# Hybrid attention encoder layer: the input projection, apart from the near values, computed from feature pairs as seven block products

## The chip, the core and the metric

The kernel runs on one core of one Trainium2 chip. Its engines are TensorE (PE, matrix products; its weight loads are listed as PEld), VectorE (DVE), ScalarE (ACT), GpSimd (POOL) and SyncE (SP), which here only starts transfers. Each engine works through its own list of instructions in order, and a wait on a semaphore holds up everything behind it on that engine. The metric is the device time of one execution in microseconds.

## The reference

One encoder layer on x of 2048 tokens by 1024 features, float32. What the change touches is the first part:

```python
h = rmsnorm(x, g_norm_mix[l])
proj = h @ w_in[l]                       # 2048x1024 by 1024x2304
qa, ka, va, qb, kb, vb = jnp.split(proj, split_at, axis=-1)
...
qb = partial_rope(qb.reshape(b, s, SWA_HEADS, HEAD_DIM), pos)   # first 16 of 64 dims
kb = partial_rope(kb.reshape(b, s, SWA_KV_HEADS, HEAD_DIM), pos)
oa = neighbourhood_attention(qa, ka, va, na_rpb[l])   # 8 heads, 2-D windows
ob = windowed_gqa_sink(qb, kb, vb, swa_sink[l])       # 8 query heads, 2 key heads
...
x = x + o @ w_out[l]
x = x + (silu(h @ w_gate[l]) * (h @ w_up[l])) @ w_down[l]
```

qa, ka and va ("near") are 512 features each, qb ("window" queries) is 512, kb and vb are 128 each.

## The kernel before

Every large product is made from float32 operands split into a high part (rounded to the fast float32 format of PE, by ACT) and a low part (the rest, by DVE), and three matmuls replace one: high by high, high by low, low by high. All matmuls of the projection have 128 rows of output and 512 columns, or 256.

The work goes in stages: projection, attention (8 rounds of two heads), output projection with the norm after it ("mix"), and the feed-forward part. Order on each engine is written out by hand; no scheduler moves anything. The projection (`project_phase`, L60) has three stages of its own.

**Near values, token by token.** For each of 16 tiles of 128 tokens, ACT sums the squares (L375), DVE makes the norm's factor and the normed tile (L455 to L462), PE turns it with eight 128x128 transposes (L541), ACT and DVE split the turned tile into `hT` (L370, L450), and PE makes 24 matmuls against the 512 value columns (`token_step`, L573 to L575). ACT copies the result (L412), SP and POOL store it. PE's list is: product of tile t, transposes of tile t + 2, product of tile t + 1.

**Near queries and keys, feature-major.** 32 steps j of 24 matmuls each (L600 to L602): 128 features by 512 tokens. ACT and DVE split each result (L430, L515, L517), SP stores both parts to `qk_scratch` (L299). `w_out` is scaled and split on the side, one of eight pieces every second step.

**Window keys and values, then window queries, token by token.** 16 steps of 16 matmuls and 16 steps of 24 matmuls. The rotation is done with tokens on the partitions, on 16 of each head's 64 columns (`rope`, L470 to L484: four short DVE instructions a tile), and PE turns the result back (`turn_tok`, L551: one or four 128x128 transposes a tile). In the same stage SP loads what attention needs first: the queries, keys and values of heads 0 and 1, between the steps (`load_ahead`, L258).

The feed-forward part (`feed_phase`, L1484) already computes its products as seven block products of sums instead of eight (`product`, L2058). It alternates between two weight matrices, so that consecutive products on PE belong to different chains.

## Time and profile before

| | us |
|---|---|
| median of 3 runs | 2220.44 (2219.46 to 2220.89) |
| profiled execution, first to last instruction | 2218.6 |
| PE busy in it | 2185.7 (99%) |
| DVE busy | 1427.1 (64%) |
| ACT busy | 929.7 (42%) |
| POOL busy | 233.5 (11%) |

The profiled execution has no time of its own beside its span; the span is 1.8 us under the median of the runs, which is what lies around it (before the first and after the last instruction). Times of a stage are read as us from the span's start. A matmul's duration (389 ns) is longer than the distance between two starts, since matmuls overlap in the array; the distance is what counts on PE. The same holds for back-to-back work of DVE and ACT to a lesser degree.

### The profile page before, as it was taken

Reading aid. Unit: us, or ns where it says so; the run is one execution under the profiler, and the core shown is the slowest. Engines: PE = TensorE matmul, PEld = TensorE weight load, DVE = VectorE, ACT = ScalarE, POOL = GpSimd, SP = SyncE. Lnnn points to the kernel's source line nnn. Section 1 sums busy time; section 2 is a strip of 40 time slices with the busy share of each in tenths; the row PEclk is TensorE's granted clock in tenths of the full one; section 3 lists DMA queues with packets and bytes.
Section 4 is the critical chain, followed back from the end, with each engine's and each line's share of the span. In section 5 each row is a group of like instructions: output and inputs, shape, how many; then the busy total and the mean of one; then the engine's idle time right before and its main releaser. Section 6 shows DMA issues by size and latency. Waiting matters only on the chain.

```text
span 2218.6 us, 33179 instructions
## 1 busy us (share of the span) xinstructions
PE 2185.7 (99%) x11464; PEld 1813.6 (82%) x11464; DVE 1427.1 (64%) x2767; ACT 929.7 (42%) x1834; POOL 233.5 (11%) x263
## 2 busy tenths in 40 slices
PE   8999999999999999999999999999999999999998
PEld 6888888788888888888888888888888887888887
DVE  4423142499888778776656568765656578575676
ACT  4423121388889643353333335333333334131343
POOL 2370001145100000011121111100000000000000
PEclk9999999999999999999999999999999999999999
DMA  7488425789974376665454558432232286353544
GB/s 229 143 241 276 148 87 155 201 221 250 222 207 142 110 229 218 232 210 194 151 196 165 196 174 302 149 118 96 92 122 81 102 321 223 114 180 103 193 147 154
DMA packets 278149, 393.46 MB, mean 177 GB/s; under 512 B 15530, under 2 KB 182578, under 8 KB 271616
## 3 DMA queue, kind: packets, MB, share of 16 engines
q1 hardware_dynamic: 269040, 366.73, 51.7%
q0 software_dynamic: 6528, 16.07, 2.4%
q10 hardware_dynamic: 2448, 8.91, 1.5%
q8 instruction: 81, 1.33, 0.2%
q14 instruction: 52, 0.43, 0.1%
HBM read 246.16 MB, written 148.70 MB: 178 GB/s over the span
## 4 chain that ended last, share of the span: by engine, by line
PE 92%; DVE 4%; issue 1%; DMA 1%; ACT 1%; DVEq 0%; ACTq 0%
PE late_psum L2089 12%; PE late_psum L2090 12%; PE late_psum L2091 12%; PE late_psum L2115 6%; PE late_psum L2117 6%; PE late_psum L2116 6%; PE late_psum L1051 4%; PE late_psum L1028 4%; PE late_psum L1433 3%; PE late_psum L573 3%; PE late_psum L575 3%; PE late_psum L574 3%; PE late_psum L1435 3%; PE late_psum L1434 3%; PE late_psum L601 3%; PE late_psum L600 3%
## 5 line engine op out<-in xcount | busy, mean ns | idle before, releaser
L2089 PE MATMUL late_psum<-ff_h,ff_ring 128*128 128x512 f32 x1232 | 479.6, 389 | 1.3 <-DVE ff_acts L1950 1.3
L2090 PE MATMUL late_psum<-ff_h,ff_ring 128*128 128x512 f32 x1232 | 479.3, 389 | 0.0
L2091 PE MATMUL late_psum<-ff_h,ff_ring 128*128 128x512 f32 x1232 | 479.3, 389 | 0.0
L2089 PEld LDWEIGHTS late_psum<-ff_h,ff_ring 128*128 128x128 f32 x1232 | 231.3, 188 | 50.1 <-DVE ff_acts L1950 2.2
L2090 PEld LDWEIGHTS late_psum<-ff_h,ff_ring 128*128 128x128 f32 x1232 | 231.3, 188 | 48.0
L2091 PEld LDWEIGHTS late_psum<-ff_h,ff_ring 128*128 128x128 f32 x1232 | 231.3, 188 | 47.8
L2115 PE MATMUL late_psum<-ff_d,ff_a 128*128 128x512 f32 x616 | 240.0, 390 | 2.1 <-DVE ff_x L2008 1.4
L2117 PE MATMUL late_psum<-ff_d,ff_a 128*128 128x512 f32 x616 | 239.7, 389 | 0.0
L2116 PE MATMUL late_psum<-ff_d,ff_a 128*128 128x512 f32 x616 | 239.7, 389 | 0.0
L2008 DVE TENSOR_TENSOR ff_x<-late_psum,ff_x 128x512 f32<-128x512 f32 x224 | 153.3, 690 | 117.1 <-PE late_psum L2117 116.5
L1908 DVE TENSOR_TENSOR ff_ring<-ff_raw,ff_ring 128x512 fp32r<-128x512 f32 x176 | 130.7, 744 | 103.2 <-ACT ff_ring L1785 103.0
L914 ACT ACTIVATE att_probs<-att_neg_scores,att_negmax 128x385 f32<-128x385 f32 (+4 forms) x256 | 161.1, 629 | 22.8 <-DVE att_negmax L962 21.9
L1800 ACT CAST ff_a<-ff_a 128x768 fp32r<-128x768 f32 (+2 forms) x96 | 81.5, 878 | 206.3 <-DMA ff_a<-acts_scratch 206.1
L1908 DVE TENSOR_TENSOR ff_ring<-ff_sums,ff_ring 128x512 fp32r<-128x512 f32 x132 | 94.5, 717 | 112.4 <-ACT ff_ring L1785 112.1
L1785 ACT CAST ff_ring<-ff_raw 128x512 fp32r<-128x512 f32 x176 | 109.3, 623 | 137.1 <-PE late_psum L2091 135.9
L1028 PE MATMUL late_psum<-ident,att_probs 128*128 128x128 f32 (+1 forms) x816 | 133.8, 277 | 10.9 <-ACT att_probs_turned L936 4.9
L2115 PEld LDWEIGHTS late_psum<-ff_d,ff_a 128*128 128x128 f32 x616 | 115.6, 188 | 27.5 <-issue 2.1
L2117 PEld LDWEIGHTS late_psum<-ff_d,ff_a 128*128 128x128 f32 x616 | 115.6, 188 | 24.1
L2116 PEld LDWEIGHTS late_psum<-ff_d,ff_a 128*128 128x128 f32 x616 | 115.6, 188 | 24.0
L936 ACT COPY att_probs_turned<-late_psum 128x384 f32<-128x384 f32 (+2 forms) x256 | 124.4, 487 | 19.1 <-PE late_psum L1028 19.0
L1028 PEld LDWEIGHTS late_psum<-ident,att_probs 128*128 128x128 f32 (+1 forms) x816 | 98.5, 140 | 39.8 <-issue 16.3
L975 DVE TENSOR_SCALAR att_probs<-att_probs,att_rtotal 128x384 f32<-128x384 f32 (+3 forms) x256 | 129.9, 508 | 0.1
(151 smaller groups left out, 3934.1 us busy)
## 6 DMA issues: line engine op xcount, KB each, us to landing
acts_scratch<-ff_acts SPq DMA_DIRECT2D x22, 1792.0 KB, 8.2
ff_a<-acts_scratch SPq DMA_DIRECT2D x24, 960.0 KB, 5.2
ff_raw<-in_w_gate SPq DMA_DIRECT2D x44, 512.0 KB, 3.8
ff_raw<-in_w_up SPq DMA_DIRECT2D x44, 512.0 KB, 4.0
ff_d<-down_scratch SPq DMA_DIRECT2D x21, 768.0 KB, 6.5
att_q_stack<-qk_scratch SPq DMA_DIRECT2D x56, 256.0 KB, 6.1
ffn_in_scratch<-mix_h_stage SPq DMA_DIRECT2D x8, 1792.0 KB, 6.2
ff_h<-ffn_in_scratch SPq DMA_DIRECT2D x14, 1024.0 KB, 8.4
```

Source lines behind the costliest of these rows:

```text
L914: nc.scalar.activation(pr[:, i, lo:hi], sn[:, i, lo:hi], ACT.Exp, bias=negmax[:, i:i + 1], scale=-1.0, accum_out=total[:, i:i + 1]).then_i ...
L936: nc.scalar.copy(turned_buffer(u)[:, 0:n], tp[:, u % 2, 0:n]).then_inc(pt_copied, 1)
L975: nc.vector.tensor_scalar(pr[:, i, c0:c0 + n], pr[:, i, c0:c0 + n], rtotal[:, i:i + 1], None, ALU.mult).then_inc(probs_done, 1)
L1028: last = pe.transpose(tp[0:rows, u % 2, j * P:(j + 1) * P], pr[:, i, c0 + j * P:c0 + j * P + rows], ident[:])
L1908: nc.vector.tensor_tensor(ff.ring[m % TURNS][:, 1], weight_of(m), ff.ring[m % TURNS][:, 0], ALU.subtract) \
L2008: nc.vector.tensor_tensor(to, down_bank(e, j), to, ALU.add).then_inc(added, 1)
L2089: pe.matmul(out_bank, whi[:, k], hhi[:, :, k], start=(k == 0 and not onto), stop=False, skip_group_check=onto)
L2090: pe.matmul(out_bank, whi[:, k], hlo[:, :, k], start=False, stop=False, skip_group_check=onto)
L2091: last = pe.matmul(out_bank, wlo[:, k], hhi[:, :, k], start=False, stop=(k == 3), skip_group_check=onto)
L2115: pe.matmul(bank, hi, dhi, start=(i == 0 and not onto), stop=False, skip_group_check=onto)
L2116: pe.matmul(bank, hi, dlo, start=False, stop=False, skip_group_check=onto)
L2117: last = pe.matmul(bank, lo, dhi, start=False, stop=(i == n - 1), skip_group_check=onto)
```

## The change

The 1792 feature columns of w_in that are not near values are reordered on the host side of the launch into seven pairs of 128 + 128 (`pair_columns`), and the input projection for them becomes a 2x2 block product: contraction halves by feature halves by token halves. Such a block product is made with seven products of sums and differences (Strassen-Winograd) instead of eight. There are 14 groups g (7 pairs for the first half of the tokens, the same 7 for the second), each with seven products j of 12 matmuls of 128x512: 98 products n = 7g + j. Pair 0 and part of pairs 1 and 2 are window queries; pair 1 also has the window keys, pair 2 the window values, pairs 3 to 6 are near queries with near keys.

- The near-value stage stays, tile by tile, in another order of tiles, but it now also makes the sums of the turned input: ACT copies parts of the turned tile (`turn_copy`), and after every second tile DVE makes four sums (`turn_sums`). For the second half of the tokens the seven operands (1792 KB for each pair of tiles) go to DRAM and come back for group 7. The seven operands of a half are split into high and low in pieces of 128x2048 (`split_hi`, `split_lo`), seven of these for the second half.
- The sums of weights are made by DVE (`weight_sums`, `last_weight_sum`: four of 128x512 a group). POOL's queue loads the weights, 1 MB a group. `pair_hi` and `pair_lo` split the weights of one product, six products ahead.
- Results are put together from partial sums: ACT copies three of them out of PSUM (`evacuate`), DVE adds to them (`join`), then ACT and DVE split the four results of a group (`result_hi`, `result_lo`).
- The rotation is done with features on the partitions: window queries are grouped so that one 128-row result holds 16 dimensions of all eight heads, and DVE makes a shuffle of partitions, two products with tables and a sum, all of 128x512 (`rope`, four times in groups 1 and 8). SP loads the tables, two of four parts at a time. The 80 transposes of rotated tiles go; 16 transposes of window values come (`turn_values`).
- `w_out` is scaled from product 59 on, one piece every four products.
- The first loads of attention move behind product 91 and later ones (`first_loads`), in smaller pieces; the last projection tile is no longer finished inside attention's first steps, and the identity matrix is no longer loaded again.

Where three places of the lists stood before, and stand now. First, DVE at the end of the near-value stage: `hT` and `x_turned` are the turned and split tile, `x_normed` the normed tile, `proj_h_stage` the sums of the turned input. Before:

```order
L450 TENSOR_TENSOR hT<-late_psum,hT 128x1024
L455 TENSOR_SCALAR msq<-ssq 128x1
L458 RECIPROCAL inv<-msq 128x1
L462 SCALAR_TENSOR_TENSOR x_normed<-x_tile,rstd,g_mix_rows 128x1024
L450 TENSOR_TENSOR hT<-late_psum,hT 128x1024
L467 TENSOR_TENSOR w_lo<-w_raw,w_hi 128x1024 x4
```

After, for an odd tile:

```order
L632 TENSOR_TENSOR x_turned<-late_psum,x_turned 128x512 x2
L641 TENSOR_TENSOR proj_h_stage<-late_psum,proj_h_stage 128x512
L642 TENSOR_TENSOR proj_h_stage<-proj_h_stage,late_psum 128x512
L644 TENSOR_TENSOR proj_h_stage<-proj_h_stage 128x512
L646 TENSOR_TENSOR proj_h_stage<-proj_h_stage 128x512
L650 TENSOR_SCALAR msq<-ssq 128x1
L653 RECIPROCAL inv<-msq 128x1
L657 SCALAR_TENSOR_TENSOR x_normed<-x_tile,rstd,g_mix_rows 128x1024
```

The four sums now stand between the low part of one tile and the norm of the next.

Second, the rotation. SP before, at the window keys and values: `v_window_scratch` is the store of values, `stage` holds the split results.

```order
L299 DMA qk_scratch<-stage_hi 128x512
L299 DMA qk_scratch<-stage_lo 128x512
L322 DMA v_window_scratch<-x_tile 128x128
L333 DMA qk_scratch<-stage_hi 128x128
L333 DMA qk_scratch<-stage_lo 128x128
L255 DMA w_raw<-in_w_in 128x2x512
```

SP after, in group 1: stage 2 holds the second result of the group (the window keys), stage 0 the third.

```order
L331 DMA qk_scratch<-stage_hi1 8x16x512
L331 DMA qk_scratch<-stage_lo1 8x16x512
L331 DMA qk_scratch<-stage_hi2 128x512
L331 DMA qk_scratch<-stage_lo2 128x512
L294 DMA rope_rows0<-in_rope 128x2x512 x2
L331 DMA qk_scratch<-stage_hi0 8x16x512
L331 DMA qk_scratch<-stage_lo0 8x16x512
```

And DVE there (c1 is the third result, c3 the second):

```order
L697 TENSOR_TENSOR proj_c1<-late_psum,proj_c1 128x512
L671 TENSOR_TENSOR proj_ring0<-proj_raw0,proj_ring0 128x512
L727 TENSOR_TENSOR stage_lo2<-proj_c3,stage_hi2 128x512
L711 STREAM_SHUFFLE rope_swapped0<-proj_c1 128x512
L713 TENSOR_TENSOR rope_swapped0<-rope_swapped0,rope_rows0 128x512
L714 TENSOR_TENSOR proj_c1<-proj_c1,rope_rows0 128x512
L716 TENSOR_TENSOR proj_c1<-proj_c1,rope_swapped0 128x512
```

The tables, loaded by POOL's queue before, are now between two stores on SP, and the third rotation stands right behind the low part of the second result.

Third, DVE where the second half of the tokens is prepared. Before, in the near keys (L517 is a result's low part, L467 a weight split, L247 a piece of `w_out`):

```order
L515 TENSOR_TENSOR stage_lo<-late_psum,stage_hi 128x8x4x16
L467 TENSOR_TENSOR w_lo<-w_raw,w_hi 128x8x128
L517 SCALAR_TENSOR_TENSOR stage_lo<-late_psum,stage_hi 128x512
L247 SCALAR_TENSOR_TENSOR w_out_parts<-w_out_raw,g_out,w_out_parts 128x1024
L517 SCALAR_TENSOR_TENSOR stage_lo<-late_psum,stage_hi 128x512 x4
```

After, in products 45 to 47 (`proj_h_second` is an operand of the second half, `ring` the split weights, c3 and c1 results):

```order
L667 TENSOR_TENSOR proj_h_second<-proj_h_second 128x2048
L697 TENSOR_TENSOR proj_c3<-late_psum,proj_c3 128x512
L671 TENSOR_TENSOR proj_ring4<-proj_w_sums,proj_ring4 128x512
L667 TENSOR_TENSOR proj_h_second<-proj_h_second 128x2048
L729 SCALAR_TENSOR_TENSOR stage_lo1<-proj_c3,stage_hi1 128x512
L689 TENSOR_TENSOR proj_w_sums<-proj_raw0,proj_w_sums 128x512
L697 TENSOR_TENSOR proj_c1<-late_psum,proj_c1 128x512
L671 TENSOR_TENSOR proj_ring5<-proj_raw1,proj_ring5 128x512
L667 TENSOR_TENSOR proj_h_second<-proj_h_second 128x2048
L727 TENSOR_TENSOR stage_lo2<-proj_c1,stage_hi2 128x8x4x16
```

Three of the long splits stand in three consecutive products, among the joins that PE waits for.

The diff, cut to its core:

```diff
+    OP_LOADS = {8: 1, 23: 0}
+    OP_LOADS.update({PER_G * HALF_GROUPS - PER_G + o - 1: o for o in range(2, SEVEN)})
+    SPLIT_AT_TILE = {13: (0, 2), 14: (0, 3), 15: (0, 4)}
+    SPLIT_AT = {0: (0, 6), 24: (1, 1), 31: (1, 0), 45: (1, 2), 46: (1, 3), 47: (1, 4), 49: (1, 5), 51: (1, 6)}
...
+    HI_AT = {ROPED: (2, 5, 6, 8), VALUES: (1, 6, 5, 9)}
+    ROPE_AT = (1, 4, 5, 7)
+    SIDES = ((0, 0), (1, 1), (0, 1), (1, 0))
+    order = sorted(((PER_G * g + HI_AT.get(kind_of(g), (1, 4, 5, 6))[i], g, i) for g in range(G) for i in range(4)))
...
+    def store_sums(u):
+        sp.wait_ge(h_summed, 4 * (u + 1))
+        sp.dma_start(sums_dram[:, :, u - 4].rearrange("o p c -> p o c"), hs[:]).then_inc(h_stored, 16)
+    def load_rope(b, turn):
+        for side, half in enumerate((0, 1) if turn == 0 else (1, 0)):
+            if turn == 0 and b == 0:
+                sp.wait_ge(v_done, NT)
+            elif turn == 0:
+                sp.wait_ge(prod_done, PER_G * HALF_GROUPS)
+            else:
+                sp.wait_ge(roped, 4 * b + side + 1)
+            cols = slice((2 * b + half) * BANK, (2 * b + half + 1) * BANK)
+            sp.dma_start(mem.p_rope[b][:, side], rope_in_dram[side].rearrange("c p s -> p c s")[:, :, cols]) \
+                .then_inc(rope_in[side], 16)
...
+    def load_op(o):
+        if o == 1:
+            sp.wait_ge(h_stored, 64)
...
+        else:
+            sp.wait_ge(prod_done, HOME_FREED[o])
+        sp.dma_start(hc[:, o, 1].bitcast(F32), sums_dram[o].rearrange("p q c -> p (q c)")).then_inc(h_in[o], 16)
...
+    def first_loads(att):
+        sp.wait_ge(prod_done, PRODUCTS - 6)
+        for slot in range(STAGES):
+            sp.wait_ge(stored[slot], max(v for r, v in stored_by.items() if r % STAGES == slot and order[r][1] < G - 2))
+        att.load_q(att.near, 0, 0)
+        sp.wait_ge(prod_done, PRODUCTS - 4)
+        att.load_k(att.near, 0, 0)
+        att.load_k(att.near, 0, 1)
+        sp.wait_ge(prod_done, PRODUCTS - 3)
+        for half in range(2):
+            sp.wait_ge(v_stored[half], 32 * NT)
+            sp.wait_ge(v_stored_by_pool[half], 32 * NT)
+        att.load_v(att.near, 0, 0)
+        att.load_v(att.near, 0, 1)
+        att.load_k(att.near, 0, 2)
+        att.load_q(att.near, 0, 1)
...
+        load_rope(0, 0)
+        for n in range(LAST_STEP + 1):
+            if n == 7 * ROPED + 6:
+                load_rope(0, 1)
+            if n == PER_G * HALF_GROUPS:
+                load_rope(1, 0)
...
+            for r, g, i in results_at(n):
+                store_result(r, g, i)
+            if n == 95:
+                first_loads(att)
...
-    def turn_hi(t):
-        act.wait_ge(turned, t + 1)
-        nc.scalar.copy(hT[:, t, 0], tp[:, t % 2, :].rearrange("p (k s) -> p k s", k=KT)).then_inc(h_hi_done, 1)
+    def turn_hi(t):
+        act.wait_ge(turned, t + 1)
+        if t >= 8 or t in (5, 7):
+            act.wait_ge(v_done, slot_before(t) + 1)
+        for half in range(2):
+            last = nc.scalar.copy(raw_part(t, half, 0), tp[:, t % 2, half * BANK:(half + 1) * BANK])
+        last.then_inc(h_hi_done, 1)
...
+    def turn_copy(t):
+        u = t // 2
+        if t < 2:
+            act.wait_ge(h_lo_done, t + 1)
+        if t == 0:
+            act.wait_ge(v_lo_done, 4)
+        elif t % 2 == 0:
+            act.wait_ge(h_summed, 4 * u)
+            if u > 4:
+                act.wait_ge(h_stored, 16 * (u - 4))
+        if t % 2 == 0:
+            nc.scalar.copy(hs[:, 0:2], tp[:, 0].rearrange("p (o c) -> p o c", o=2)).then_inc(h_copied, 1)
+        else:
+            nc.scalar.copy(hs[:, 5], tp[:, 1, BANK:2 * BANK]).then_inc(h_copied, 1)
...
+    def pair_hi(n):
+        g, j = place(n)
+            act.wait_ge(sums_made, 4 * g + {2: 2, 3: 1, 4: 3, 5: 4}[j])
+        if RING // 2 <= n < RING:
+            act.wait_ge(v_done, NT)
+        if n >= RING:
+            act.wait_ge(prod_done, n - RING + 1)
+        nc.scalar.copy(ring[n % RING][:, 0], weight_of(n)).then_inc(w_hi_done, 1)
+    def evacuate(n):
+        g, j = place(n)
+        if j == 3 and g >= 1:
+            if kind_of(g - 1) == VALUES:
+                act.wait_ge(v_turned, 2 * (g // HALF_GROUPS) + 1)
+            else:
+                all_low(act, g - 1, 1)
+        act.wait_ge(prod_done, n + 1)
+        if j in (0, 2, 3):
+            nc.scalar.copy({0: c0, 2: c1, 3: c3}[j][:], bank_of(g, j)).then_inc(copied, 1)
...
-    def turn_lo(t):
-        dve.wait_ge(h_hi_done, t + 1)
-        nc.vector.tensor_tensor(hT[:, t, 1], tp[:, t % 2, :].rearrange("p (k s) -> p k s", k=KT), hT[:, t, 0],
-                                ALU.subtract).then_inc(h_lo_done, 1)
+    def turn_sums(u):
+        t = 2 * u + 1
+        s3, s4, s2, s6 = (sum_of(t, o) for o in (3, 4, 2, 6))
+        dve.wait_ge(h_copied, t + 1)
+        nc.vector.tensor_tensor(s3, tp[:, 1, 0:BANK], hs[:, 0], ALU.subtract).then_inc(h_summed, 1)
+        nc.vector.tensor_tensor(s4, hs[:, 5], tp[:, 1, 0:BANK], ALU.subtract).then_inc(h_summed, 1)
+        dve.wait_ge(h_summed, 4 * u + 1)
+        nc.vector.tensor_tensor(s2, hs[:, 5], s3, ALU.subtract).then_inc(h_summed, 1)
+        dve.wait_ge(h_summed, 4 * u + 3)
+        nc.vector.tensor_tensor(s6, hs[:, 1], s2, ALU.subtract).then_inc(h_summed, 1)
...
+    def split_lo(b, o):
+        nc.vector.tensor_tensor(op_of(b, o)[:, 1], op_sums(b, o), op_of(b, o)[:, 0], ALU.subtract).then_inc(op_lo_done, 1)
...
+    def weight_sums(g):
+        nc.vector.tensor_tensor(sums[:, 0], a21, a22, ALU.add).then_inc(sums_made, 1)
+        dve.wait_ge(sums_made, 4 * g + 1)
+        nc.vector.tensor_tensor(sums[:, 1], sums[:, 0], a11, ALU.subtract).then_inc(sums_made, 1)
+        nc.vector.tensor_tensor(a21, a11, a21, ALU.subtract).then_inc(sums_made, 1)
...
+    def join(n):
+        g, j = place(n)
+        first, to = {1: (1, c0), 4: (3, c3), 5: (2, c1)}[j]
+        dve.wait_ge(copied, 3 * g + first)
+        dve.wait_ge(prod_done, n + 1)
+        nc.vector.tensor_tensor(to[:], bank_of(g, j), to[:], ALU.add).then_inc(summed, 1)
...
-        nc.vector.tensor_tensor(rope_c[:, 0:heads, :], v[:, :, 0:ROPE], cos, ALU.mult).then_inc(rope_step, 1)
-        nc.vector.tensor_tensor(rope_s[:, 0:heads, 0:HALF], v[:, :, HALF:ROPE], sin[:, :, 0:HALF],
...
-        nc.vector.tensor_tensor(v[:, :, 0:ROPE], rope_c[:, 0:heads, :], rope_s[:, 0:heads, :],
...
+    def rope(g, i):
+        dve.wait_ge(rope_in[side], 16 * (2 * b + (1 if i < 2 else 2)))
+        nc.vector.stream_shuffle(swapped[:], v[:], [lane ^ 8 for lane in range(32)]).then_inc(rope_step, 1)
+        dve.wait_ge(rope_step, 3 * nth + 1)
+        nc.vector.tensor_tensor(swapped[:], swapped[:], table[:, side, 1], ALU.mult).then_inc(rope_step, 1)
+        nc.vector.tensor_tensor(v[:], v[:], table[:, side, 0], ALU.mult).then_inc(rope_step, 1)
+        dve.wait_ge(rope_step, 3 * nth + 3)
+        nc.vector.tensor_tensor(v[:], v[:], swapped[:], ALU.add).then_inc(roped, 1)
...
+        for n in range(LAST_STEP + 1):
+            g, j = place(n)
+            if n < PRODUCTS and j in (1, 4, 5):
+                join(n)
+            if n + RING < PRODUCTS:
+                pair_lo(n + RING)
+            if n in SPLIT_AT:
+                split_lo(*SPLIT_AT[n])
+            for r, gg, i in results_at(n):
+                result_lo(r, gg, i)
+            for gg, i in ropes_at(n):
+                rope(gg, i)
+            if j == 2 and g + 1 < G:
+                weight_sums(g + 1)
+            if j == 4 and g + 1 < G:
+                last_weight_sum(g + 1)
+            if n - 2 in OUT_AT:
+                out_weights_lo(OUT_AT[n - 2])
...
-            for k in range(KT):
-                if j == 0:
-                    wait_low(pe, 4 + k // 2)
-                pe.matmul(mm[:, j % 4, :], w_hi[:, k, cols], hT[:, tiles, 0, k, :], start=(k == 0), stop=False)
-                pe.matmul(mm[:, j % 4, :], w_hi[:, k, cols], hT[:, tiles, 1, k, :], start=False, stop=False)
-                last = pe.matmul(mm[:, j % 4, :], w_lo[:, k, cols], hT[:, tiles, 0, k, :], start=False,
+    def product(n):
+        g, j = place(n)
...
+        if g >= 2 and j in (1, 3):
+            pe.wait_ge(summed, 3 * (g - 2) + {1: 1, 3: 3}[j])
+        if j in (2, 4, 5):
+            pe.wait_ge(copied, 3 * g + {2: 1, 4: 2, 5: 3}[j])
+        if j == 6:
+            pe.wait_ge(summed, 3 * g + 2)
+        pe.wait_ge(w_lo_done, n + 1)
...
+        for k in range(4):
+            pe.matmul(out, whi[:, k], hhi[:, :, k], start=(k == 0 and not onto), stop=False, skip_group_check=onto)
+            pe.matmul(out, whi[:, k], hlo[:, :, k], start=False, stop=False, skip_group_check=onto)
+            last = pe.matmul(out, wlo[:, k], hhi[:, :, k], start=False, stop=(k == 3), skip_group_check=onto)
```

## Rows read from the trace of the kernel before

**Rows 1.** The page: span, and engines of the chain of work that ended last.

```profile
span 2218.6 us, 33179 instructions
...
PE 92%; DVE 4%; issue 1%; DMA 1%; ACT 1%; DVEq 0%; ACTq 0%
```

**Rows 2.** Busy time by stage: span, PE, PEld, DVE, ACT, POOL, PEclk, DMA, GB/s.

```profile
291.00:435.00 144.00, 143.30 (x731) 120.44 (x729) 51.85 (x186) 32.07 (x73) 8.23 (x8) 1.00 0.58 156
435.00:447.00 12.00, 9.20 (x54) 7.17 (x55) 10.99 (x37) 8.64 (x26) 5.42 (x5) 0.72 0.34 88
```

**Rows 3.** Timeline of PE: start, duration, instruction; transposes, then first product of the queries.

```profile
66.63 1.03 PE L541 MATMUL late_psum<-ident,x_normed 128*128 128x128 f32 x8
...
72.96 1.04 PE L541 MATMUL late_psum<-ident,x_normed 128*128 128x128 f32 x8
...
116.49 0.39 PE L600 MATMUL late_psum<-hT,w_hi 128*128 128x512 f32 x1
```

**Rows 4.** Timeline of PE where attention begins.

```profile
430.84 0.60 PE L551 MATMUL late_psum<-ident,x_tile 128*128 128x128 f32 x4
431.19 0.41 PE L1015 MATMUL late_psum<-att_k_stack,att_q_stack 128*128 128x352 f32 x1
...
437.08 0.55 PE L1028 MATMUL late_psum<-ident,att_probs 128*128 128x128 f32 x3 [2.27 <-DMA ident<-in_ident]
```

**Rows 5.** Timeline of PE in the feed-forward products.

```profile
1002.06 0.39 PE L2089 MATMUL late_psum<-ff_h,ff_ring 128*128 128x512 f32 x1
...
1002.74 0.39 PE L2089 MATMUL late_psum<-ff_h,ff_ring 128*128 128x512 f32 x1
```

**Rows 6.** Timeline of ACT, one tile of the near values.

```profile
66.82 0.59 ACT L412 COPY stage_hi<-late_psum 128x512 f32<-128x512 f32 x1 [2.72 <-PE late_psum L575]
67.70 1.02 ACT L370 CAST hT<-late_psum 128x1024 fp32r<-128x1024 f32 x1 [0.29 <-PE late_psum L541]
...
68.61 1.06 ACT L375 ACTIVATE x_normed<-x_tile 128x1024 f32<-128x1024 f32 x1
```

**Rows 7.** Timeline of DVE, the same tile.

```profile
68.75 1.23 DVE L450 TENSOR_TENSOR hT<-late_psum,hT 128x1024 fp32r<-128x1024 f32 x1 [3.33 <-ACT hT L370]
...
70.07 0.17 DVE L458 RECIPROCAL inv<-msq 128x1 f32<-128x1 f32 x1
70.50 1.29 DVE L462 SCALAR_TENSOR_TENSOR x_normed<-x_tile,rstd,g_mix_rows 128x1024 f32<-128x1024 f32 x1 [0.27 <-ACT rstd L377]
```

**Rows 8.** Timeline of DVE, back-to-back work of 128x512 in the feed-forward products.

```profile
1019.79 0.68 DVE L1935 TENSOR_TENSOR ff_gate<-late_psum,ff_gate 128x512 f32<-128x512 f32 x1
1020.39 0.68 DVE L1908 TENSOR_TENSOR ff_ring<-ff_raw,ff_ring 128x512 fp32r<-128x512 f32 x1
```

**Rows 9.** Groups of instructions on DVE, 860 to 1400 us: the split of 128x2048.

```profile
L1913 DVE TENSOR_TENSOR ff_h<-ff_h 128x2048 fp32r<-128x2048 f32 x14 | 33.1, 2364 | 7.8 <-ACT ff_h L1789 7.8
```

**Rows 10.** Timeline of ACT in the feed-forward products.

```profile
1008.43 0.59 ACT L1811 COPY ff_gate<-late_psum 128x512 f32<-128x512 f32 x1 [1.61 <-PE late_psum L2091]
1008.92 0.62 ACT L1785 CAST ff_ring<-ff_raw 128x512 fp32r<-128x512 f32 x1
```

**Rows 11.** DMA issues up to 440 us: count, KB each, median us to landing.

```profile
w_raw<-in_w_in SPq DMA_DIRECT2D x18, 512.0 KB, 6.9
x_tile<-in_x ACTq DMA_DIRECT2D x16, 512.0 KB, 4.3
```

**Rows 12.** DMA issues of the whole page.

```profile
ffn_in_scratch<-mix_h_stage SPq DMA_DIRECT2D x8, 1792.0 KB, 6.2
```

**Rows 13.** Timeline of SP: the issue of one load of keys.

```profile
404.65 0.60 SPq L840 DMA_DIRECT2D att_k_stack<-qk_scratch  x1
```

**Rows 14.** Timeline of DVE in attention's first steps.

```profile
433.19 0.52 DVE L962 CUSTOM_DVE_ANT_0 att_neg_scores<-late_psum,bias 128x352 f32<-128x352 f32 x1
...
435.12 1.51 DVE L975 TENSOR_SCALAR att_probs<-att_probs,att_rtotal 128x352 f32<-128x352 f32 x1
...
441.64 0.40 DVE L975 TENSOR_SCALAR att_probs<-att_probs,att_rtotal 128x352 f32<-128x352 f32 x1
```

938 lines of the change are left out of this document (510 added, 428 removed).

## The prediction

> **What bounds the kernel now.** Read the page's head and chain first: PE is on 92% of the chain that ended last [rows 1], so a change pays only if it takes time out of PE's list, and costs whatever it makes PE wait. Then the busy time by stage: from 291 to 435 us, the stage of the rotated features, PE is busy 143.3 of 144.0 us, DVE 51.9 and ACT 32.1 [rows 2]. There PE never waits; the others have two thirds of the time free. Then the timelines, for what one instruction costs back to back. Two starts of the same line of a product are 0.68 us apart, which is three matmuls of 512 columns [rows 5]: 0.227 us each, so a product of 12 takes 2.72 us and one of 24 takes 5.44. DVE's instructions of 128x512 start 0.60 us apart and end 0.68 after their start [rows 8]; ACT's start 0.49 apart and last 0.6 [rows 10]; DVE's split of 128x2048 takes 2.36 [rows 9]. ACT's of that size is not shown; its 1024 columns take 1.02 [rows 6], so 2.05. I add 0.04 for a handover between engines: ACT's result is read by DVE 0.03 after its end [rows 6, 7].
>
> **What goes from PE's list.** The first product of the queries starts at 116.49, attention's first score at 431.19 [rows 3, 4]: 314.7 us. In its place stand 98 products of 2.72 us, 266.6, and 16 transposes; four of these take 0.35 us before the next row [rows 4], 1.5 in all. Saved, if PE never waits: 46.6 us. Everything else is what PE waits for.
>
> **The near-value stage.** A tile takes PE 6.33 us [rows 3]: eight transposes, 0.87, and 5.44. Let the value product of an odd tile t end at 0. PE turns tile t + 2, whose rows are there at 0.91 (ACT starts on them 0.88 after the start of its copy of the values, [rows 6]). ACT: two halves until 1.9, its copy of 512 until 2.4, the squares of tile t + 3 (0.96 and a read of the sum) until 3.5. DVE: two low halves from 2.45 until 3.7; four sums, two of which wait for the one before, until 6.2; then the norm: mean and inverse 0.35, ACT's root, and the 1.29 of the last step, which starts 0.43 after the inverse did [rows 7]: 8.1. PE wants to turn tile t + 3 at 6.33: it waits 1.8 us. In an even tile the sums are missing and the copy is twice as long: 6.0, in time. Odd tiles with a tile left to norm: t = 1, 3 to 11, six: 10.8 us. For the second half of the tokens the staged sums are also stored, 1792 KB, and ACT's next copy of an even tile waits for it. A store of this size lands 6.2 us after its issue [rows 12]; issued at 6.3, it is down at 12.5, where ACT wants to go on at 10.0 (the delay above included): 2.4 us more, for three tiles, 7.2. **18.0 us** together. Lower end 8 (the sums slip into gaps, only the stores wait), upper end 28 (each wait and landing half as long again).
>
> **Into the products.** DVE comes out of the tiles with three splits of 2.36, three weight sums and six weight splits. Counted from the end of tile 13, the last weight split that ACT must make before it copies the result of product 0 out waits for a sum DVE finishes at 18.2; the copy ends at 19.4, product 2 was due at 17.3; product 4 waits 1.8 more behind ACT. **3.9 us** (0 to 8).
>
> **A plain group.** Seven products are 19.0 us. DVE has seven weight splits, three joins, four sums, four low parts: 18 x 0.60 = 10.8; ACT 14 x 0.50 = 7. Followed through their lists step by step, with each one's waits for the other, both keep up; the join behind product 4 ends 0.7 after it, product 6 wants it at 2.7. Nothing, and `w_out`'s pieces (1.3 us on DVE each fourth product) fit as well.
>
> **The two rotation groups.** Counted from the end of product 8. The third rotation stands on DVE right behind the low part of the second result, which ends at 15.6. Its table is asked for by SP only after SP has stored that low part: issue at 16.5, and 512 KB land 4.3 us (tiles of x) to 6.9 us (weights) later [rows 11]; I take 5.5. So DVE starts it at 22, and is through at 24.8. (A rotation is a shuffle and three instructions with two handovers; no row shows a shuffle. It is bounded by 0.17, a one-column instruction, and 2.36, the one of 2048 [rows 7, 9]; I take the 0.68 of its own size, 2.8 for a rotation.) ACT stands behind it: high part of the third result 25.4, one weight split, and only then the copy of product 14's result, 26.4. Product 16, which adds onto that bank, was due at 19.1: PE waits 7.3 us, and 0.9 more before product 18. Twice, with two pieces of `w_out` in the second one that cost 1.0 before the transposes of values: **17.4 us** (5, if the tables are down in time and only DVE's load counts, to 24).
>
> **Splits of the second half's operands.** Products 24 and 31 each get one split of 2.36 on DVE ahead of a join: 0.7 us each. Products 45, 46, 47, 49 and 51 get five. Counted from the end of product 43, DVE is through with step 45 at 11.0, with step 46 at 18.5, with step 47 at 25.4, and ACT, which waits for each join, copies product 49's result out only at 24.1; product 51 was due at 19.9. Waits of 0.7, 4.3, 2.3, 0.4 and 2.2 at products 48, 51, 53, 54 and 55. With the first two: **11.3 us** (3 to 18).
>
> **Into attention.** Before, queries and keys lay ready, and DVE took the first score 2.0 us after PE's first [rows 4, 14]. Now SP comes to these loads after the store of the result of product 95, 1.4 us before the last product ends, and each issue takes 0.60 [rows 13]. Ten stand up to the last key the first score needs: the last is issued 4.6 us after the last product, and lands some 4.8 later (between 4.3 and 6.9, [rows 11]): 9.4, which is 7.4 later than before. Given back: the bias sums of POOL, under which DVE's scaling took 1.51 us for 0.40 [rows 14], are nearly over by then, about 3 us, and the last tile's low part 0.6. **+3.8 us** (0 to 8).
>
> **The sum.** 46.6 saved; 18.0 + 3.9 + 17.4 + 11.3 + 3.8 = 54.4 lost: 7.8 us slower. Against the profiled span of 2218.6 that is 2226.4; the runs' median lies 1.8 above the span: 2228.2. The terms' ends give 16 to 86 us lost, which all together is unlikely.
>
> **Rivals.** *The queues take it up* (faster). Handovers are shorter and the tables land before DVE wants them: then the rotation groups cost 5 and the splits, spread by PE's own lag, 4: 12.4 + 7.3 less, about 12 us faster, 2208. For it: DVE is idle two thirds of that stage now [rows 2], and its total load in the products, some 70%, leaves room. Against: PE's tolerance is one product, 2.7 us, since all seven belong to one chain, and the order of SP's list fixes the late table. *Half of it*: one of these two goes away but not the other, 2216 to 2225, taken as 2220. *The clock falls* (slower still). After PE's idle 2.27 us before 437.08 [rows 4] the stretch to 447 has a granted clock of 0.72 [rows 2], that is 0.56 of it, 6.7 us, at 1.2 GHz and the rest at 2.4. The change makes six waits of 2.3 us and more inside PE-bound work (three stores, two tables, one at product 51). If each is followed by 6.7 us at half clock, each costs up to 3.4 more, less where DVE is what is late: some 15 us, 2243. Against: the waits of the near-value stage stand between long products, and the wait before 437 is a single case. The Trainium skill ("TensorE: Matmul & The Clock Gate", section "HAM oscillation — how this bites in real kernels") says that waits between bursts of matmuls put the array back to half clock each time; by that rule this rival would be the forecast. The trace agrees for the wait before 437. That the change would not do what it says has no place here: the products are counted in the list.
>
> **Chances.** Forecast (2222 to 2236) 0.40; the clock falls 0.17; half of it 0.20; the queues take it up 0.23. A difference under 0.2% (4.4 us) is no change here. The forecast is slower but for 0.02 at its lower end, and the clock's case wholly; the last is faster; "half of it" is 0.18 no change and 0.01 to either side: faster 0.24, same 0.20, slower 0.56. The forecast's own range is 2222 to 2236; to hold eight in ten the range reaches to the rivals on both sides: 2207 to 2243.
>
> **What would show it.** Right: about 266.6 us of product time in 98 products at 0.227 a matmul; PE waits of about 1.8 us before the transposes of every second tile, larger from tile 10 on; DVE idle for about 6 us on a transfer of `rope_rows` before the third shuffle of each rotation group; a wait of 4 us before product 51; PE idle for about 9 us before the first score, waiting for `att_k_stack`. Wrong: no wait on `rope_rows` (SP reaches the load earlier than I count, or it lands faster), or near-value tiles that stay at 6.33; either alone takes the time towards no change, both make it faster. Granted clock under 1.00 between 20 and 420 us would speak for the fourth case.

## The result, and the profile after

The changed kernel takes 2267.22 us (median of 4 runs, 2266.05 to 2269.49) against 2220.32 for the kernel before in the same comparison (2219.46 to 2220.89): ratio 1.0214, 95% interval 1.0200 to 1.0229. The forecast was 2228 with 2207 to 2243 as its range, so the sign was right, and the size was short by 39 us. The profiled span is 2266.0 us, 47.4 more than before. The page's chain answers to [rows 1]:

```profile
PE 80%; DVE 7%; DMA 5%; issue 3%; ACT 3%; SPq 1%; DVEq 0%; ACTq 0%
```

PE had 92% of that chain; 12 points of it now belong to others. Busy time by stage answers to [rows 2] (span, PE, PEld, DVE, ACT, POOL, PEclk, DMA share, GB/s); the stretches are most of the near values, the two halves of the products, the gap before attention, and its start:

```profile
23.00:141.00 118.00, 101.09 (x444) 81.38 (x443) 58.20 (x100) 50.66 (x96) 29.77 (x59) 0.90 0.56 169
147.00:300.00 153.00, 140.83 (x606) 114.67 (x605) 101.74 (x149) 66.63 (x107) 44.86 (x76) 0.97 0.71 218
300.00:460.00 160.00, 139.13 (x579) 112.12 (x578) 103.26 (x151) 66.86 (x107) 5.47 (x7) 0.94 0.72 238
462.00:474.00 12.00, 0.21 (x1) 0.00 (x0) 1.15 (x2) 1.88 (x2) 12.00 (x11) 0.64 0.98 209
474.00:520.00 46.00, 36.84 (x298) 30.89 (x299) 31.84 (x114) 30.49 (x81) 15.63 (x15) 0.87 1.09 254
```

PE, which before had no idle time in the products, now stands still for 12.2 and 20.9 us of their two halves, and the granted clock is under 1.00 in every stretch. Three marks divide the 47.4. The first product starts at 146.72, where 116.49 stood [rows 3]: 30.2 later. The first score comes at 474.17, against 431.19 [rows 4]: 43.0. By the 40th score 48.2 us are lost, and from there to the end it stays between 47.7 and 48.2. So the near-value stage costs 30.2, the products nearly nothing net (+0.8 up to the start of their last row), and the start of attention 12.0 and then 5 more.

PE's rows with their waits, in the near-value stage, in the products and in attention:

```profile
85.53 1.12 PE L792 MATMUL late_psum<-ident,x_normed 128*128 128x128 f32 x8 [1.92 <-DVE x_normed L657]
95.94 1.29 PE L792 MATMUL late_psum<-ident,x_normed 128*128 128x128 f32 x8 [2.22 <-DVE x_normed L657]
...
202.32 0.80 PE L853 MATMUL late_psum<-proj_h_first,proj_ring 128*128 128x512 f32 x1 [8.09 <-ACT proj_c L540]
307.36 0.47 PE L853 MATMUL late_psum<-proj_h_second,proj_ring 128*128 128x512 f32 x1 [3.87 <-issue]
358.31 0.79 PE L853 MATMUL late_psum<-proj_h_second,proj_ring 128*128 128x512 f32 x1 [7.73 <-ACT proj_c L540]
372.51 0.50 PE L853 MATMUL late_psum<-proj_h_second,proj_ring 128*128 128x512 f32 x1 [3.60 <-ACT proj_c L540]
427.14 0.50 PE L853 MATMUL late_psum<-proj_h_second,proj_ring 128*128 128x512 f32 x1 [2.83 <-ACT proj_c L540]
474.17 0.63 PE L1243 MATMUL late_psum<-att_k_stack,att_q_stack 128*128 128x352 f32 x1 [11.96 <-issue]
...
499.07 0.76 PE L1243 MATMUL late_psum<-att_k_stack,att_q_stack 128*128 128x480 f32 x1 [5.18 <-DMA att_q_stack<-qk_scratch]
```

These are the waits the prediction named, nearly all at its places: about 1.9 before every second tile (4, 6, 8 and 10), larger ones from the stores on (tiles 11, 13 and 15), 8 before products 16 and 65 (counted from 0), 3.9 before product 51. All waits of about 0.4 us and more in the near-value stage add up to 17.3 (18.0 forecast, with a wait on ACT of 0.4), those in the products to 32.8 (32.6 forecast). And still 27 us more are gone: 12.9 in the near-value stage (30.2 less 17.3), for which a granted clock of 0.90 over 123.7 us has 12.4, and 14.2 in the products, whose 315.1 us are 268.1 of work at 0.227 us a matmul, 32.8 of waits and this rest, at a clock of 0.94 to 0.97.

Tile by tile it shows: behind the wait before tile 4 the clock falls, behind that before tile 6 it does not. The same work takes 7.98 us in the first and 6.42 in the second (one line for each, same columns):

```profile
37.83:45.81 7.98, 7.98 (x32) 6.59 (x33) 2.80 (x5) 3.24 (x6) 2.29 (x4) 0.79 0.82 259
54.24:60.66 6.42, 6.42 (x33) 5.30 (x33) 2.80 (x5) 3.24 (x6) 1.35 (x3) 1.00 0.58 161
```

That is where one is tempted to stop: the rival "the clock falls" seems to be the whole answer. The experiments say that it is a part, and a smaller one than 27 us.

### The profile page after: what moved, and what is told of

Its sections match the earlier page's. It is cut to its first block, busy times and chain, and to the rows that moved or that the text cites. A ratio compares the mean times of both kernels' runs of the same rounds, so it can differ in the third digit from the quotient of the medians.

```text
span 2266.0 us, 33068 instructions
## 1 busy us (share of the span) xinstructions
PE 2166.6 (96%) x11168; PEld 1787.7 (79%) x11168; DVE 1565.9 (69%) x2892; ACT 1012.7 (45%) x1967; POOL 243.7 (11%) x275
## 4 chain that ended last, share of the span: by engine, by line
PE 80%; DVE 7%; DMA 5%; issue 3%; ACT 3%; SPq 1%; DVEq 0%; ACTq 0%
PE late_psum L2334 11%; PE late_psum L2336 11%; PE late_psum L2335 11%; PE late_psum L2360 6%; PE late_psum L2361 6%; PE late_psum L2362 6%; PE late_psum L1278 4%; PE late_psum L1255 3%; PE late_psum L1676 3%; PE late_psum L1678 3%; PE late_psum L1677 3%; PE late_psum L853 2%; PE late_psum L855 2%; PE late_psum L854 2%; PE late_psum L1243 2%
## 5 line engine op out<-in xcount | busy, mean ns | idle before, releaser
L2030 ACT CAST ff_ring<-ff_sums 128x512 fp32r<-128x512 f32 x132 | 81.5, 619 | 113.6 <-PE late_psum L2336 108.2
L1243 PE MATMUL late_psum<-att_k_stack,att_q_stack 128*128 128x384 f32 (+3 forms) x256 | 112.5, 439 | 19.4 <-issue 12.0
```

What stands on the lines that cost most here:

```text
L1243: pe.matmul(out, q, kind.keys(k_st[:, e, 0, :], t), start=True, stop=False)
L2030: nc.scalar.copy(ff.ring[m % TURNS][:, 0], weight_of(m)).then_inc(w_hi_done, 1)
```

## Experiments

**Two repairs that each take away one thing.** Theory: VectorE's order costs the 1.9 us, the clock behind them the rest. In the first run the norm goes ahead of the sums:

```
             turn_lo(t + 2)
-            if t % 2:
-                turn_sums((t + 2) // 2)
         if t + AHEAD < NT:
             normed_tile(t + AHEAD)
+        if t + 2 < NT and t % 2:
+            turn_sums((t + 2) // 2)
```

> The changed kernel, with VectorE's order in the near-value stage turned round: the norm of tile t+3 ahead of the four sums of the pair (t+1, t+2). Theory A (waits and clock): the four waits of 1.9 us before the transposes of tiles 4, 6, 8 and 10 go (7.7 us), and with them most of what the clock lost in that stage (the first product is 30.2 us later than before, 17.3 of it waits and 12.4 half clock): 2251 (2247 to 2257), first product at about 131. Theory B (waits alone, the granted clock of that stage has another cause): 2259 (2257 to 2261) and a mean granted clock there that stays at 0.90. Theory C (the sums now make the copies and the 1792 KB stores later, and the three waits at tiles 11, 13 and 15 grow by as much): 2267.

Measured: 2266.56 us (ratio to before 1.0211, 1.0194 to 1.0228): no change. Theory C. Up to 80 us the stage has no wait over 0.5 us and a granted clock of 1.00, but then PE stands 8.4, 8.3 and 6.6 us, and the first product comes at 147.45. ACT's copies of an even tile and SP's stores of that kernel:

```profile
84.64 1.01 ACT L489 COPY proj_h_stage<-late_psum 128x1024 f32<-128x1024 f32 x1 [8.47 <-DMA proj_in_scratch<-proj_h_stage]
107.84 1.01 ACT L489 COPY proj_h_stage<-late_psum 128x1024 f32<-128x1024 f32 x1 [8.40 <-DMA proj_in_scratch<-proj_h_stage]
```
```profile
76.07 0.39 SPq L282 DMA_DIRECT2D proj_in_scratch<-proj_h_stage  x1
98.24 0.38 SPq L282 DMA_DIRECT2D proj_in_scratch<-proj_h_stage  x1
```

Copy, sums, store, copy again is a ring through one buffer. Here it turns in 23.2 us (84.64 to 107.84), where PE wants a pair of tiles in 12.7 (twice the 6.33 of [rows 3]). The same two rows in the changed kernel:

```profile
91.66 1.02 ACT L489 COPY proj_h_stage<-late_psum 128x1024 f32<-128x1024 f32 x1 [3.90 <-DMA proj_in_scratch<-proj_h_stage]
110.35 1.01 ACT L489 COPY proj_h_stage<-late_psum 128x1024 f32<-128x1024 f32 x1 [3.53 <-DMA proj_in_scratch<-proj_h_stage]
```
```profile
102.77 0.38 SPq L282 DMA_DIRECT2D proj_in_scratch<-proj_h_stage  x1
```

18.7 us for a turn: 11.1 from the copy to the store's issue, 7.6 from there to the next copy. (The turn ahead of it takes 19.9, from a copy at 71.81, the one behind it 18.6, to a copy at 128.99.)

With the norm first the same two parts are 13.6 and 9.6 us. The first is longer for theory C's reason, the sums that come later, and for another that it did not name: behind a wait of 8.4 us PE's product runs at half clock (tile 11 takes 8.4 us for 6.4), and the sums wait for the turned tile behind it. Why the stores also took 2 us longer was not tested.

The second run leaves all waits and fills them:

```
             value_step(t)
+            if t + 2 in FILL:
+                if t + 1 >= 4:
+                    pe.wait_ge(tok_done, t - 2)
+                for _ in range(FILL[t + 2]):
+                    pe.matmul(mm[:, (t + 1) % 4, :], raw_part(t, 0, 0)[:, 0:P], w_hi[:, 0], start=True, stop=True)
```

> The changed kernel with nothing moved: only that TensorE, where it waited for x_normed in the near-value stage, does useless products of 128x512 instead (8 each before tiles 4, 6, 8 and 10, 10 before 11, 2 before 12, 15 before 13, 12 before 15; 71 in all, 16.1 us at 0.227 each; their sums are overwritten). Clock theory: the same length of work in the place of the waits, but TensorE isn't idle, so the granted clock of the stage goes back from 0.90 to 1.00 and some 12 us come back: 2255 (2252 to 2260). Waits theory (what isn't a wait is contention or slower work elsewhere, and the clock in the records is no cause): no change, 2267 (2265 to 2270).

Measured: 2267.79 us (1.0216, 1.0199 to 1.0233): no change. The stretches that answer to the first three of the windows above:

```profile
23.00:141.00 118.00, 111.12 (x533) 90.05 (x532) 61.24 (x103) 52.92 (x99) 31.03 (x62) 1.00 0.60 181
147.00:300.00 153.00, 139.66 (x596) 113.64 (x596) 101.70 (x151) 65.82 (x106) 41.98 (x71) 0.96 0.70 219
300.00:460.00 160.00, 140.96 (x572) 114.03 (x572) 101.52 (x147) 64.63 (x106) 8.15 (x9) 0.91 0.71 234
```

In the near-value stage the clock is back at its full level, and ACT's copies still come 19.3 us apart (87.57, 106.91). The first product is at 141.11, 3.5 to 5.6 us earlier than in three kernels whose near-value stage is the same without the fill (144.57, 145.34, 146.72). Against the changed kernel's 146.72, 1.0 of the 5.6 us stands before tile 4 already. 3.1 are won from tile 4 to tile 10, nearly all in tiles 4 and 8, which ran behind a fallen clock (7.98 and 8.01 us, now 6.42 and 6.41). From tile 10 on, where the ring turns, only 1.5 are won, though the granted clock of the changed kernel's last 61.2 us (0.86) has some 8.6 us there. So the clock costs its full price where nothing but PE is late, and in the ring it is mostly hidden.

At the end nothing is left of the 5.6 us, and that is not the near-value stage's doing. The products, which the edit does not touch, have the same waits (32.5 us) but a lower granted clock than in the changed kernel (0.96 and 0.91 for 0.97 and 0.94), and take 318.4 us in place of 315.1. Why the clock fell oftener there is open. So no change at the end does not say that the clock has no price.

**The store in two.** What the ring needs free for the next copy is 512 KB of the 1792:

```
+    def store_copies(u):
+        sp.wait_ge(h_copied, 2 * u + 1)
+        sp.dma_start(sums_dram[0:2, :, u - 4].rearrange("o p c -> p o c"), hs[:, 0:2]).then_inc(copies_stored, 16)
...
             if u > 4:
-                act.wait_ge(h_stored, 16 * (u - 4))
+                act.wait_ge(copies_stored, 16 * (u - 4))
+        elif u > 4:
+            act.wait_ge(h_stored, 16 * (u - 4))
```

> The norm ahead of the four sums on VectorE, and the 1792 KB store of a pair's sums in two: the two copied operands (512 KB) as soon as the first copy of the pair stands, the five others after the sums. The first copy of the next pair then waits only for the small store. Theory A (two limits, each of which hid the other: VectorE's order costs 1.9 us at every second tile, the store costs the pair's cycle its length): both waits go, a tile takes 6.4 us again, the first product is at 119 (117 to 122) instead of 146.7, and all but a few us of it reach the end: 2242 (2236 to 2250). Theory B (what is won there is waited for again in the products or at the start of the attention, as with the filled waits, where 5.6 us at the first product were 2.3 at the 400th score): 2256 to 2262.

> The store in two as in the run above, but VectorE's order left as it was. Theory A (two limits): the three long waits at tiles 11, 13 and 15 (8.4 us) go and two more of 1.9 us show at tiles 12 and 14, so the stage is 5 us shorter and its granted clock stays near 0.90: 2262 (2259 to 2265). Theory B (the store alone is the limit, and the order of VectorE only hides in it): as the run above.

Measured, both edits: 2241.97 us (1.0101, 1.0085 to 1.0118). Store in two alone: 2258.90 (1.0169, 1.0152 to 1.0186), first product at 136.43. With norm first alone at 2266.56, that is 25 us for both, 8 and 0 for each: two limits, of which each hides the other. In the kernel with the store in two alone no ring is in the way, and all six waits of the prediction stand there, 1.9 each, before tiles 4, 6, 8, 10, 12 and 14. Behind four of them the clock falls and the tile takes 8.0 us, behind tiles 8 and 14 it does not and takes 6.4. Tiles 12 and 14 of that kernel:

```profile
101.75:109.77 8.02, 8.02 (x33) 6.55 (x33) 2.80 (x5) 3.23 (x6) 1.99 (x4) 0.79 0.97 309
118.19:124.60 6.41, 6.41 (x32) 5.28 (x33) 2.80 (x5) 3.24 (x6) 1.35 (x3) 1.00 0.94 313
```

Its near-value stage is 19.9 us longer than before: 11.5 of waits, 6.4 of half clock (1.6 for each of four tiles) and 2 more. Of the kernel with both, the windows near 23 to 117, ACT's copies and PE's last transposes and first product:

```profile
23.00:117.00 94.00, 92.90 (x461) 76.36 (x459) 60.32 (x102) 54.56 (x99) 31.75 (x63) 1.00 0.71 226
```
```profile
89.75 1.02 ACT L500 COPY proj_h_stage<-late_psum 128x1024 f32<-128x1024 f32 x1 [0.30 <-DVE proj_h_stage L657]
102.84 1.01 ACT L500 COPY proj_h_stage<-late_psum 128x1024 f32<-128x1024 f32 x1 [0.27 <-DVE proj_h_stage L657]
```
```profile
107.12 1.09 PE L803 MATMUL late_psum<-ident,x_normed 128*128 128x128 f32 x8 [0.19 <-DVE x_normed L668]
...
118.97 0.39 PE L864 MATMUL late_psum<-proj_h_first,proj_ring 128*128 128x512 f32 x1
```

The ring turns in 13.1 us, and the first product is 27.8 us earlier than in the changed kernel. The granted clock is 1.00: the repair took the half clock away together with the waits. (The profile is that of the fastest of the four runs, 2235.64; the kernel with all repairs, below, has its first product at 119.18 in a run near its median.)

**The late table.** The second tables of the rotations are asked for one side at a time, as soon as a side is free (`load_rope(b, 1, (0,))` ahead of the results of product 9, `(1,)` ahead of those of 12, in each half).

> The changed kernel with the second turn of the rope tables asked for one side at a time, as soon as each side's first use is over (ahead of the results of products 9 and 12 of each half instead of behind the results of product 12). My theory: the waits of 8.1 and 7.7 us in the two rotation groups shrink to 1 or 2 us each, as ScalarE's copies are then held by VectorE's work alone, and the half clock behind them (about 3.4 and 5.1 us lost) goes too: 2247 (2243 to 2253). Rival 1 (the waits go, the clock doesn't): 2255. Rival 2 (the four rotations on VectorE take as long as the table was late, so the wait only changes its name): 2263 to 2267.

Measured: 2255.89 us (1.0167, 1.0150 to 1.0184), 11.3 less. DVE's row in the changed kernel, and in this one:

```profile
197.76 0.01 DVE L711 LOAD_MASK_SELECT rope_swapped<-proj_c  x1 [6.63 <-DMA rope_rows<-in_rope]
197.78 0.72 DVE L711 STREAM_SHUFFLE rope_swapped<-proj_c 128x512 f32<-128x512 f32 x1
```
```profile
190.88 0.01 DVE L717 LOAD_MASK_SELECT rope_swapped<-proj_c  x1 [1.13 <-DMA rope_rows<-in_rope]
```

PE's two waits go from 8.09 and 7.73 to 2.60 and 1.39 (0.71 and 0.70 more a little later). My theory of the waits stands; with the half clock it gave 2247, without it 2255, and 2255.9 is what was measured. That the time is the second one's is partly luck. Around the two places (products 15 to 18 and 64 to 66) the loss goes from 20.2 us to 6.5, which is 13.7 and more than the waits alone, so the half clock behind them did come back; 3.1 of it was lost again later, at `w_out` (a wait of 4.91 for 3.60 before product 68) and before product 51.

**Filling everything.** The fill above, and 120 more matmuls and 90 transposes ahead of six of the products and of the first score. (The expectations from here on count the products from 1, this text from 0, as the prediction does.)

> The changed kernel, with useless work on TensorE in nearly all of its waits up to the first score: the 71 products of 128x512 of the near-value stage, 120 more ahead of products 17, 52, 56, 66, 69 and 87 of the 98 (35, 16, 9, 33, 15 and 12 of them), and 90 transposes of the identity between the last product and the first score. Nothing waits less. Clock theory: some 14 us of the products' 315 are half clock behind those waits and come back, with a few at the start of the attention: 2250 (2244 to 2257). Rival (where TensorE runs at half clock behind a wait it only catches up less with what it waits for next, so the end hardly moves): 2263 to 2267.

Measured: 2264.04 us (1.0194, 1.0177 to 1.0211), its interval overlapping that of the changed kernel. Its windows:

```profile
147.00:300.00 153.00, 146.37 (x642) 119.03 (x641) 102.34 (x151) 63.12 (x103) 41.98 (x71) 1.00 0.69 216
300.00:460.00 160.00, 151.07 (x649) 122.51 (x649) 101.48 (x147) 67.09 (x108) 7.44 (x8) 0.98 0.72 237
462.00:474.00 12.00, 9.30 (x85) 9.10 (x84) 0.69 (x1) 1.29 (x2) 12.00 (x12) 1.00 1.08 238
```

The rival of this run holds, though not at every place: the mean granted clock of the whole kernel goes from 0.983 to 0.994, and 3 us are won. Count at each place what the products there take over 2.72 us each. At the two late tables that is 10.1 and 10.2 us in the changed kernel, 9.8 and 8.7 here: the full clock gives back 0.3 and 1.4. At the wait before product 86 it is 5.3 and 8.0. There the changed kernel runs at half clock for a while, and this one, at full clock, meets a new wait for ACT before product 88:

```profile
432.29 0.79 PE L861 MATMUL late_psum<-proj_h_second,proj_ring 128*128 128x512 f32 x1 [2.23 <-ACT proj_c L540]
```

So there ACT sets the pace and hides the clock. From product 50 to 55 it is 9.0 and 11.2 us, but at products 55 and 65 no wait was left behind the fill, so there it may have cost something itself. (The profile is that of the slowest of the four runs, 2268.25.) So what the half clock costs in the products as a whole is not shown by this run: at the late tables it is a part of the loss, at product 86 it is not.

**The start of attention.** The first loads go ahead of the stores of product 95's result, and one wait is added, for that store, before PE's first transposes of probabilities:

```
+            if n == 95:
+                first_loads(att)
             for r, g, i in results_at(n):
                 store_result(r, g, i)
-            if n == 95:
-                first_loads(att)
```

> The changed kernel with the first loads of the attention (queries 0, keys 0 to 2, values 0 and 1) ahead of the stores of the result of product 95 instead of behind them on SP, and one wait more for that store before the first turned probabilities. Theory A (SP's order): the first of them is issued at 454.4 instead of 460.9, so the first score comes 6.5 us earlier: 2260.5 (2257 to 2263). Theory B (the transfers themselves: the 16 queues are busy to 0.95 and more from 445 on, 2 MB has to land first): 1 or 2 us at most, 2266.

Measured: 2261.74 us (1.0192, 1.0175 to 1.0209), 5.5 less. Its first score:

```profile
468.29 0.63 PE L1244 MATMUL late_psum<-att_k_stack,att_q_stack 128*128 128x352 f32 x1 [7.94 <-issue]
```

Queries are issued at 452.70 instead of 460.91, 8.2 us earlier, and 4.0 of the 11.96 go (most of the rest of the gain at this mark is an earlier first product, 144.57 for 146.72, which the edit does not touch). So both theories have a part: SP's order, and transfers with the queues full. SP's eight issues for the first keys still take 0.60 us each, the last at 466.80, and it lands 7.2 us later, just before the first score. Behind them the queues are full: the next four keys cost SP 4.45 us, a mask that took 0.61 in the kernel before takes 10.18, and the landings from 440 to 520 are long:

```profile
468.64 4.45 SPq L1050 DMA_DIRECT2D att_k_stack<-qk_scratch  x4
...
487.64 10.18 SPq L1086 DMA_DIRECT2D att_win_mask<-in_swa_mask  x1
```
```profile
att_k_stack<-qk_scratch SPq DMA_DIRECT2D x16, 256.0 KB, 8.5
att_q_stack<-qk_scratch SPq DMA_DIRECT2D x14, 256.0 KB, 9.3
```

**All repairs.** Norm first, store in two, tables by side, and the first loads ahead with only queries 0 and keys 0 and 1.

> All repairs together: norm ahead of the sums, store in two, rope tables asked for by side, and the first loads of the attention (queries 0, keys 0 and 1) ahead of the store of the result of product 95, the rest behind it. Additive theory: 25 us from the near-value stage, 11.3 from the rope tables and 5.5 to 7 from the loads, as measured one by one: 2225 (2219 to 2232), a few us over the kernel before. Rival (the 16 queues, at 0.7 of their time in the products and 1.0 at the start of the attention, take back part of it): 2235 to 2245.

Measured: 2223.90 us (1.0018, 1.0009 to 1.0028). The gains of the single runs, 25.3 + 11.3 + 5.5 = 42.1, add up to the 43.3 found here within the scatter of the medians (the four runs of a kernel lie up to 8 us apart): the losses were independent, and little was taken back.

**The rest.** What PE still waits for in that kernel, its largest waits in the products:

```profile
273.81 0.77 PE L875 MATMUL late_psum<-proj_h_second,proj_ring 128*128 128x512 f32 x1 [3.81 <-issue]
...
334.33 0.79 PE L875 MATMUL late_psum<-proj_h_second,proj_ring 128*128 128x512 f32 x1 [4.78 <-ACT proj_c L562]
```

Three runs tried the two causes I saw for these, and the loads of attention once more. The edits: `n - 2 in OUT_AT` becomes `n - 3` on ACT and DVE (and the store `n - 4`); the operands' loads move from step `42 + o - 1` to `42 + o - 2`; both; and both with `first_loads` at step 92.

> All repairs as before, and ScalarE's and VectorE's work on the output weights one product step later behind their load (three steps instead of two; the store with it). Theory: the waits of 4.8 and 3.3 us at products 69 and 87 are ScalarE standing at w_out_raw, which its DMA brings 6 us late, with the copy that TensorE needs behind it; both go: 2217 (2214 to 2220). Rival (the DMA is late by more than a product step of 2.7 us, or the next copy is late for VectorE's sake): 2221 to 2224.

> All repairs as before, and the loads of the second half's operands 2 to 6 one step earlier in SP's order, ahead of the results of the product before. Theory A (SP stood behind a store): the first three are issued at once, 2 product steps late; with 5 us more of lead the waits of 3.8, 0.6 and 2.2 us at products 52, 54 and 56 go: 2219 (2216 to 2222). Theory B (ScalarE's and VectorE's work, 1.9 and 2.3 us for each of the five splits within seven products, is the limit, as the prediction had it): 2223.

> The two changes of the runs above together: 2213 (2209 to 2218) if both theories hold, which is faster than the kernel before; 2220 to 2224 if neither does.

> The run above, with the first loads of the attention moved from product step 95 to 92, the last two parts of the near masks behind the queries, and the keys ahead of the stores of the result of step 92. Theory A (SP's order still holds the keys back by 4 us): first score 4 us earlier, 2209 (2206 to 2214). Theory B (the 16 queues carry 1.0 and more of their time from 418 to 500, so what is asked for earlier lands no earlier in sum): as the run above, with the wait moved from the first score to the second round of queries.

Measured: 2225.26 (1.0028, 1.0017 to 1.0038), 2225.00 (1.0019, 1.0010 to 1.0029), 2222.32 (1.0011, 1.0001 to 1.0020) and 2224.25 us (1.0022, 1.0013 to 1.0031). What I hoped for came in none of them; each time the rival held, within 2 us. With the later step ACT no longer waits for the load of `w_out` but for the store of the piece before, which I had moved later too, and PE waits 4.23 before the transposes of values instead of 4.78 before product 68:

```profile
334.85 1.15 ACT L598 ACTIVATE w_out_parts<-w_out_raw,g_out 128x1024 fp32r<-128x1024 f32 x1 [3.29 <-DMA w_out_scratch<-w_out_parts]
```

With the earlier operands the wait of 3.81 is 3.32; DVE's splits then stand right behind ACT's, two of them here:

```profile
264.70 2.29 DVE L689 TENSOR_TENSOR proj_h_second<-proj_h_second 128x2048 fp32r<-128x2048 f32 x1 [1.12 <-ACT proj_h_second L535]
271.88 2.29 DVE L689 TENSOR_TENSOR proj_h_second<-proj_h_second 128x2048 fp32r<-128x2048 f32 x1 [1.10 <-ACT proj_h_second L535]
```

Both together are some 1.6 us better than without, within what the two intervals leave open. No version beats the kernel before; the best is 0.1% behind it.

## Why the prediction was right in its sign and wrong in its size

- *What goes from PE's list, 46.6.* Right: the matmuls of the products start 0.227 us apart. The kernel with everything repaired starts its products at 119.18 and the last row of them at 424.22: 305.0 us, of which 268.1 are work, 25.8 waits and the rest mostly half clock, where 314.7 stood.
- *The near-value stage, 18.0; measured 30.2.* This is the first step that failed. By tile, and against the kernel with both repairs: the four late norms up to tile 10 cost 8.1 (7.2 in the sum), the half clock behind two of them 3.3 (nothing in the sum), and from tile 10 on 16.3 are lost (10.8 in the sum). 2.5 are left even with both repairs (nothing in the sum). For the stores I took the landing (6.2, measured 7.1 in the median) against the moment at which ACT wants to go on, once, and called the rest a wait of 2.4. But copy, sums, store and next copy are a ring, and the late copy makes the next store late: its three turns are 19.9, 18.7 and 18.6 us against the 12.7 that two tiles take. The waits seen on PE add up to only 17.3, since PE at half clock arrives later and waits less: the agreement with 18.0 was no confirmation.
- *Into the products, 3.9.* Right: the first five products lose 3.8. Half of it is a wait of 1.95 before product 2, the other half stands as half clock behind it; in the kernel with both repairs it is two waits, 1.96 and 1.28, before products 2 and 4.
- *The two rotation groups, 16.4 of the 17.4.* Right in mechanism: 8.1 and 7.7 on PE, DVE idle 6.6 and 6.3 us on the table. The shuffle, which no row of before showed, takes 0.73 us (0.68 taken). With the half clock and gaps around them the two places lose 20.2.
- *`w_out`'s pieces, 1.0 of the 17.4.* The second step that failed. A plain group was to carry them for nothing: I counted their work on DVE and never the landing of their load. ACT stands 5.6 us at it twice, with the copy that PE needs right behind it, and PE waits 3.6 and 2.8 us before products 68 and 86. With the half clock around them the two places lose 11.2. This is read from the trace; the later step that was to repair it only changed the transfer at which ACT stands.
- *Splits of the second half's operands, 11.3.* Right: 8.6 us of waits at products 27, 34, 48, 51, 53 and 55 (1.03, 0.55, 0.55, 3.87, 0.45, 2.17), 12.0 with what stands behind them.
- *Into attention, 3.8; measured 12.0 at the first score and 16.7 from the 40th on* (47.7 less the 31.0 up to the last product). The third step that failed. The order and the issue were right: the last key is issued 4.6 us after the last product, as forecast. It lands 7.2 us later, not 4.8. The 5.6 us taken off (2.0 for the first score before, 3.0 and 0.6 given back) did not come: the lag shrinks by 2.2 up to the 30th score and then grows by 7, when PE waits 5.18 for queries that SP issued at 484.83 and that took 14.1 us to land. I gave each load the landing of a single one, while SP asks for 28 loads from 460.9 to 487, in a stretch in which the DMA share is 0.98 to 1.09.
- *The rival of the clock.* Its sign in the records was right: behind the waits the granted clock falls, to 0.90 of full speed in the mean between 23 and 141 us. It was left out of the forecast's sum, and at its places it costs 1.6 us a tile where nothing else is late. The price of the whole was wrong, mine of 15 us (for six waits; the short ones before the tiles were not among them) and the one that the records suggest, 27: a clock kept at 1.00 by useless work gave 5.6 us at the first product and 0 at the end of one run, 3 in the other. The Trainium skill ("TensorE: Matmul & The Clock Gate", section "HAM oscillation — how this bites in real kernels"), by which waits between bursts of matmuls put the array back to half clock each time, is borne out in part: the clock fell behind three of the four waits of 1.9 us of the changed kernel, not behind the one before tile 6. Where the array at half speed stands in the shadow of another engine, as in the ring and at product 86, its time is not lost.

The forecast was short by 39 us, and 39.5 are found: 12.2 in the near-value stage (30.2 for 18.0), 12.9 at the start of attention (16.7 for 3.8), and 14.4 in the products, where the losses that I had at 32.6 come to 47.0, the difference of 315.1 and 268.1. Of these last 10.2 are at `w_out`'s pieces and 3.8 at the two late tables. What the half clock alone is worth in the products stays open.

## What to carry to other kernels

When a buffer is written, stored and written again, compute the length of one turn of the ring and set it against the time that the bound engine takes for the same work; the wait seen once at one place is not the loss. A stretch at half clock is a loss only if the engine in it is the one that everything waits for. Fill the wait with useless work before naming the clock a cause, and read the gain at the end of the stage that was filled: the end of the kernel can hide it, as the clock of a later stage differs from run to run. And a repair that does nothing alone may be half of one that does: here 0 and 8 us apart, 25 together.
